# The last layer of a three-block kernel on 256 instead of 272 tokens

## The reference

```
h = jnp.concatenate([meta, x], axis=1)
for layer in range(DEPTH):                       # DEPTH = 2
    g = norm_gains[layer]
    h = h + 0.5 * rmsnorm_3(swiglu(rmsnorm_3(h, g[0]), w_ffn_in[layer, 0], w_ffn_out[layer, 0]), g[1])
    hn = rmsnorm_3(h, g[2])
    if layer < N_A_LAYERS:
        mix = gla_mixer(...)
    else:
        mix = swa_mixer(hn, swa_w_q[b], swa_sinks[b], swa_w_out[b], k_sh, v_sh, cos, sin)
    h = h + rmsnorm_3(mix, g[3])
    h = h + 0.5 * rmsnorm_3(swiglu(rmsnorm_3(h, g[4]), w_ffn_in[layer, 1], w_ffn_out[layer, 1]), g[5])
    if layer == N_A_LAYERS - 1:
        k_sh, v_sh = shared_kv(h, kv_norm, w_kv, cos, sin)
return h[:, N_META:]
```

## Time and profile before

| | |
|---|---|
| time, median of 3 runs | 3398.8 us (3395.87, 3398.80, 3410.93) |
| profiled execution, span from first to last instruction | 3401.5 us |
| PE, weight loads, DVE, ACT, POOL busy | 96%, 92%, 52%, 45%, 27% of the span |
| chain that ended last | PE 85%, DVE 7%, ACT 4% |
| mean granted clock of TensorE | 0.975 of full speed |
| HBM read | 479 MB, 141 GB/s over the span |

### The profile page before, as it was taken

The page is one execution under the profiler, slowest core; times in us unless marked ns, Lnnn a source line. Parts: engine busy times, 40 slices in busy tenths (PEclk is TensorE's granted clock), DMA queues, the critical chain, the costliest instruction groups (busy, mean ns, idle before and its releaser), DMA issues.

```text
span 3401.5 us, 65089 instructions
## 1 busy us (share of the span) xinstructions
PE 3265.4 (96%) x27906; PEld 3136.6 (92%) x27906; DVE 1780.3 (52%) x3018; ACT 1514.1 (45%) x2528; POOL 910.9 (27%) x486
## 2 busy tenths in 40 slices
PE   8998999999899999998989999999999999999999
PEld 8997999997788999988978899999889999986998
DVE  5456555548664545356576444454535446445543
ACT  5444444544323544447454544444424435443442
POOL 3321232332343322322211222233113223221222
PEclk9999999999899999999999999999999999998999
DMA  6552354554202555543433445455324544530353
GB/s 224 186 171 78 137 186 168 186 174 155 69 3 87 185 174 179 186 139 114 154 106 115 134 150 176 145 177 175 110 69 142 174 162 154 175 131 26 134 175 114
DMA packets 133391, 484.61 MB, mean 142 GB/s; under 512 B 14959, under 2 KB 17151, under 8 KB 132399
## 3 DMA queue, kind: packets, MB, share of 16 engines
q1 hardware_dynamic: 131120, 470.25, 41.1%
q0 software_dynamic: 1984, 10.19, 0.9%
HBM read 479.34 MB, written 1.05 MB: 141 GB/s over the span
## 4 chain that ended last, share of the span: by engine, by line
PE 85%; DVE 7%; ACT 4%; issue 2%; POOL 1%; DMA 0%; SPq 0%; DVEq 0%; ACTq 0%; POOLq 0%
PE ps L182 84%; DVE lo L159 1%; ACT arena L179 1%; ACT hi L179 1%; PE ps L190 1%; DVE tmp L167 1%; DVE arena L159 1%; ACT L179 1%; DVE arena L167 1%; DVE yT L167 1%; POOL small L159 0%; ACT hh L179 0%; DVE xT L159 0%; DVE small L176 0%; POOL arena L159 0%
## 5 line engine op out<-in xcount | busy, mean ns | idle before, releaser
L182 PE MATMUL ps<-hh,lo 128*128 128x256 f32 (+1 forms) x4624 | 1313.2, 286 | 0.0
L182 PE MATMUL ps<-hh,hi 128*128 128x256 f32 (+1 forms) x4336 | 1240.9, 289 | 31.3 <-DVE hl L167 8.8
L182 PE MATMUL ps<-hl,hi 128*128 128x256 f32 (+1 forms) x4336 | 1197.2, 286 | 1.2 <-DVE hl L159 1.2
L159 POOL TENSOR_TENSOR lo<-raw,hi 128x1024 fp32r<-128x1024 f32 x271 | 689.4, 2544 | 1800.3 <-ACT hi L179 1800.1
L179 ACT ACTIVATE hi<-raw 128x1024 fp32r<-128x1024 f32 x814 | 852.2, 1051 | 440.6 <-PE ps L182 326.4
L159 DVE TENSOR_TENSOR lo<-raw,hi 128x1024 fp32r<-128x1024 f32 x543 | 700.1, 1293 | 551.8 <-ACT hi L179 531.4
L182 PEld LDWEIGHTS ps<-hh,lo 128*128 128x128 f32 x4624 | 884.8, 191 | 0.0
L182 PEld LDWEIGHTS ps<-hh,hi 128*128 128x128 f32 x4336 | 830.6, 192 | 43.6 <-ACT arena L179 12.4
L182 PEld LDWEIGHTS ps<-hl,hi 128*128 128x128 f32 x4336 | 809.1, 191 | 1.6 <-DVE hl L159 1.4
L182 PE MATMUL ps<-hfh,lo 128*128 128x256 f32 (+1 forms) x1760 | 499.0, 284 | 0.0
L182 PE MATMUL ps<-hfh,hi 128*128 128x256 f32 (+1 forms) x1520 | 430.8, 283 | 0.0
(11 more groups left out here) (366 smaller groups left out, 3939.6 us busy)
## 6 DMA issues: line engine op xcount, KB each, us to landing
raw<-in_l_ffn_w_gate SPq DMA_DIRECT2D x88, 512.0 KB, 3.5
raw<-in_l_ffn_w_up SPq DMA_DIRECT2D x88, 512.0 KB, 3.6
raw<-in_l_ffn_w_down SPq DMA_DIRECT2D x88, 512.0 KB, 3.5
raw<-in_g SPq DMA_DIRECT2D x88, 512.0 KB, 3.5
raw<-in_u SPq DMA_DIRECT2D x88, 512.0 KB, 3.5
raw<-in_d SPq DMA_DIRECT2D x88, 512.0 KB, 3.5
raw<-in_ffn_w_gate SPq DMA_DIRECT2D x44, 512.0 KB, 3.4
raw<-in_ffn_w_up SPq DMA_DIRECT2D x44, 512.0 KB, 3.5
```

The lines of the kernel that those rows point to most:

```text
L159: return self.e.tensor_tensor(o, a, b, op)
L182: return self.e.matmul(o, a, b, start=first, stop=final, skip_group_check=loose)
```

## The change

The three last stages run with T = 256. `K.T`, which the exit norms read when they are made, is set to 256 for them. The sixteen-row attention of `Swa`, with its buffers, semaphores and waits, is gone. `Rope` gets its width as an argument: `Shared` keeps 272, and the keys and values of the learned rows are still computed. The norm that `ffn3(1, 0)` takes over from `Shared` keeps 272 columns, too.

```diff
     def scale(self, act):
         act.wait_ge(*self.norm.spr(0))
-        act.act(self.K.rstd[:, 2, 0:self.T], self.norm.out, ACT.Copy).then_inc(self.rs.h, 1)
+        act.act(self.K.rstd[:, 2, 0:self.norm.T], self.norm.out, ACT.Copy).then_inc(self.rs.h, 1)
...
-        pe.mm(bank[:, 0:T3], self.K.c("turn"), src).then_inc(self.rm.h, 1)
+        pe.mm(bank[:, 0:self.T], self.K.c("turn"), src).then_inc(self.rm.h, 1)
...
-        self.rope = Rope(K, 2, "sh", K.sig)
+        self.rope = Rope(K, 2, "sh", K.sig, T)
...
-        sg, T = K.own, T3
+        sg, T = K.own, T1
...
-        K, ps, T = self.K, self.K.ps, T3
+        K, ps, T = self.K, self.K.ps, T1
...
-            if i == 14:
-                self.meta_scores(pe)
-            if i == 17:
-                self.meta_turn(pe)
-            if i == 19:
-                self.meta_values(pe)
         pe.wait_ge(*self.ol(15))
-        pe.wait_ge(*self.m8(0))
...
-            if i == 15:
-                act.wait_ge(*self.m2(0))
-                act.act(self.st2[2], self.st2[2], ACT.Exp)
-                act.act(self.S2[0:16], self.S2[0:16], ACT.Exp).then_inc(self.m3.h, 1)
...
-        act.act(self.qs[:, j % 4, :], bank[:, 0:T3], ACT.Copy, scale=0.125).then_inc(self.rope.qs.h, 1)
+        act.act(self.qs[:, j % 4, :], bank[:, 0:T1], ACT.Copy, scale=0.125).then_inc(self.rope.qs.h, 1)
...
-            if i == 16:
-                self.meta_probs(dve)
...
-            if i == 14:
-                self.meta_max(dve)
-        dve.wait_ge(*self.mh(0))
-        dve.tt(self.mix[1][:, :, T1:T3], ps[7][:, 256:384].rearrange("p (u t) -> p u t", u=8),
-               self.mix[0][:, :, T1:T3].bitcast(F32), ALU.subtract).then_inc(self.m8.h, 1)
...
-        return Ffn(K, T3, f"g3_{a}{b}", f"u3_{a}{b}", f"d3_{a}{b}", entry(K, T3, prev, "norm_gains_3", a * 6 + 4 * b),
+        T = K.T = T1 if a else T3
+        return Ffn(K, T, f"g3_{a}{b}", f"u3_{a}{b}", f"d3_{a}{b}", entry(K, T, prev, "norm_gains_3", a * 6 + 4 * b),
                    rms("norm_gains_3", a * 6 + 4 * b + 1, True, True))
...
-        lambda p: Swa(K, Lazy(K, T3, p, "norm_gains_3", 8, False), rms("norm_gains_3", 9, False, False, K.Hf)),
+        lambda p: Swa(K, Lazy(K, T1, p, "norm_gains_3", 8, False), rms("norm_gains_3", 9, False, False, K.Hf)),
```

More of the change, by code:

```diff
@@ L3704, with __init__ @@
 class Rope:
-    def __init__(self, K, n, name, sig):
-        self.K = K
+    def __init__(self, K, n, name, sig, T):
+        self.K, self.T = K, T
         self.qs, self.rm, self.t1, self.t2 = [sig(name + "_" + s, n) for s in ("in", "rot", "cos", "sin")]
@@ L3720, in dve @@
         dve.wait_ge(*self.rm(j))
-        dve.tt(t2, bank[:, 0:T3], sin, ALU.mult).then_inc(self.t2.h, 1)
+        dve.tt(t2, bank[:, 0:self.T], sin, ALU.mult).then_inc(self.t2.h, 1)
         dve.wait_ge(*self.t2(j))
@@ L3885, in __init__ @@
         self.t1, self.t2 = buf(4 * T, 4, T), buf(2 * T, 2, T)
-        self.S2, self.P2 = buf(256, 16, 16), buf(256, 16, 16)
         self.mix = (K.sqR, K.over("swal", K.pos[0], 8, T))
@@ L3889, in __init__ @@
         self.kD, self.V = K.kD3, K.V3
-        self.rope = Rope(K, 8, "sw", sg)
+        self.rope = Rope(K, 8, "sw", sg, T)
         self.rq, self.tb = sg("sw_q", 8), sg("sw_tab", 1)
@@ L3895, in __init__ @@
             K.sig(x, 16) for x in ("scores", "rowmax", "exps", "probs", "turned", "pta", "pv", "oh", "ol")]
-        (self.m0, self.m1, self.m2, self.m3, self.m4, self.m5, self.m6, self.m7, self.m8, self.mh) = [
-            sg("sw_m" + str(i), 1) for i in range(10)]
         self.st = [(K.small[:, 64 + 4 * w:66 + 4 * w], K.small[:, 66 + 4 * w:68 + 4 * w]) for w in range(16)]
-        self.st2 = [K.small[0:16, 320 + 16 * x:336 + 16 * x] for x in range(3)]
         self.down = Down(K, T, "swa_out", self.mix, 8, lambda k: self.ol(2 * k + 1), spare=spare)
@@ L3951, in product @@
         return self.K.ps[6 + j % 2 if j < 4 else 7]
[L3953 to L3981, removed]
     def scores(self, pe, w):
@@ L4038, in act @@
     def act(self, act):
-        K, W, ps, T = self.K, self.K.W, self.K.ps, T3
+        K, W, ps, T = self.K, self.K.W, self.K.ps, T1
         self.entry.act(act)
@@ L4096, in dve @@
         dve.wait_ge(*self.entry.norm.spr(0))
-        dve.mark(dve.tt(self.cos, K.c("cos"), self.entry.norm.out, ALU.mult))
-        dve.tt(self.sin, K.c("sin"), self.entry.norm.out, ALU.mult).then_inc(self.tb.h, 1)
+        dve.mark(dve.tt(self.cos, K.c("cos")[:, 0:T], self.entry.norm.out, ALU.mult))
+        dve.tt(self.sin, K.c("sin")[:, 0:T], self.entry.norm.out, ALU.mult).then_inc(self.tb.h, 1)
         dve.wait_ge(*self.tb(0))
@@ L4168, in probs @@
         dve.tt(s, s, bc(den, 144), ALU.mult).then_inc(self.pr.h, 1)
[L4170 to L4194, removed]
     def pool(self, pool):
```

## The result

The changed kernel takes 3362.77 us (median of 4 runs, 3358.51 to 3369.05), the kernel before 3400.36 us (4 runs). The ratio is 0.9896, with a 95% interval of 0.9877 to 0.9916: 1.0% faster, 35 us by the ratio. A second measurement on another occasion gave 0.9898 (0.9878 to 0.9918). The profiled span is 3361.2 us, 40.3 us less than before.

A forecast was written before the change was run, and what follows sets the result against it. PE was taken as the bound, by the distance between matmul starts; 13.8 + 16.7 + 8.9 + 0.3 = 39.7 us off the 3398.8 us median gives 3359.1, with one microsecond less gain 3360 us; range 3349 to 3371.

The forecast's parts named there:

- Width of the wide matmuls: Three late stages: a matmul of 272 columns costs 7.5 ns more than one of 256; 26.6 us over 3552 matmuls.
- The estimate of 2.1 ns: Gain per wide matmul for sixteen columns, from the skill's 81 ns at 128 and 131 at 512 columns; time 3379 us.
- Width hardly pays: Rival: the pair of weight load and matmul sets the distance, not the columns; 3387 us, chance 0.02.
- Stage (1,0): Feed-forward stage behind the shared keys and values: 11.9 us width, 0.4 sums, 1.5 exit; 13.8 us shorter.
- Stage (1,1): Last feed-forward stage: 16.7 us shorter, from its 256-token twin in the first block, 193.85 against 210.52 us.
- the last 1.8 us: Stage (1,1): rest of 16.7 us beyond parts summing to 14.9, mostly a clock dip behind the 24 small entry sums.
- Attention stage: Sliding-window attention: 3.3 width, 0.8 entry sums, 0.9 chain, 1.9 exit, 2.0 sixteen-row part; 8.9 us shorter.
- the 3.90 us: Attention entry: DVE's first addition shows no progress while POOL works; said to stay, up to 3.9 us more if gone.
- The sixteen-row part: Separate attention of the sixteen rows: scores 0.6, transposes nothing, value products 1.2, last DVE operation 0.2; 2.0 us.
- Exit and projection: End of the attention stage: exit 1.9 us shorter, 192 output-projection matmuls each 7.5 ns cheaper.
- Clock: Attention stage: removed scores may add time at 1.2 GHz, at most 2.5 us; rival of more frequent falls 3364 us, chance 0.09.
- Supply: Late feed-forward stages: weight supply keeps up at 118 ns; rival that it takes over 3384 us, chance 0.02.

The follow-up runs named there:

- experiment 1: Against the kernel before: only the last feed-forward stage at 256 tokens, stage (1,0) and attention at 272; 3378.75 us, ratio 0.9948.
- experiment 2: Against the kernel before: both late feed-forward stages at 256 tokens, attention kept at 272 with its sixteen-row part; 3370.02 us, ratio 0.9926.
- experiment 4: Changed kernel with wide matmuls of 240 columns in stage (1,0) and 192 in (1,1), one execution; 112.2 ns per matmul at both, attention stage 128.4 us.
- experiment 5: Changed kernel with wide matmuls of 128 columns in stage (1,0) and 64 in (1,1), one execution; 3502.5 us.
- experiment 3: Against the kernel before: the sixteen-row attention left out, all widths kept at 272; ratio 1.0014.
- experiment 7: Changed kernel with holding matmuls on PE before the transposes in the last steps of the attention loop; 3353.88 us, ratio 0.9874.

## Why the prediction was right, step by step

The forecast was 3360 us with 3349 to 3371; measured 3362.8. The sum of 39.7 us stands against 40.3 in the span, but its parts did not all come out, and the closeness of the total is in part luck.

*Width of the wide matmuls: right.* 7.5 ns each, in both stages and in experiments 1 and 2. The estimate of 2.1 ns that the prediction worked out from the Trainium skill, "TensorE: Matmul & The Clock Gate", section "Back-to-back issue gap", is refuted between 256 and 272 columns only; experiments 4 and 5 show a floor of PE's own just below, at 112 ns (and at 128 columns 111.7 ns, where the prediction cites 81). "Width hardly pays" would have been right for a cut from 240 columns on.

*Stage (1,0): right,* 13.8 us forecast and 13.8 measured.

*Stage (1,1): right in size, its smallest part misread.* 16.63 us against 16.7. I had put the last 1.8 us down mostly to a dip of the clock behind the 24 small sums. Experiment 3 has these 24 sums with no dip, and its stage takes 209.84 us to the first update in place of 210.52. The dip is worth 0.7 us. Another part belongs to POOL's two powers. The chain of waits of the kernel of experiment 3, at the entry of its last stage:

```profile
3197.09 3.42 POOL small L159 x2
...
3200.55 3.50 PE ps L182 x24
```

They last 3.42 us while DVE forms weight corrections, and PE, not slowed by the dip, waits for them by 0.57 us. With 256 tokens there is one power and PE's rows show no wait behind it. The dip had only hidden this wait. That is 0.7 and 0.6 of the 1.8 us; the last 0.5 us no row here places.

*Attention stage: too small,* 8.9 us forecast and 12.6 measured. That lies just outside the 5 to 12 us that the prediction had set as the sign of being right here. One term was mis-sized: the 3.90 us in which DVE's first addition shows no progress were to stay. In the changed kernel they are gone at that place, and 2.00 us of such a stretch stand three additions later. DVE's rows of the changed kernel in order of time:

```profile
3038.68 0.86 DVE L159 TENSOR_TENSOR arena<-arena 128x256 f32<-128x256 f32 x1 [1.11 <-POOL arena L159]
...
3041.64 2.11 DVE L159 TENSOR_TENSOR arena<-arena 128x256 f32<-128x256 f32 x1
```

So the fourth rotation came 5.9 us earlier within the stage (18.6 in place of 24.5 us) against 2.5 expected; at the first turned tile 5.1 us are left. I had named up to 3.9 us for this and excluded it, with the reason that POOL issues the same work; experiment 2 shows that the same work can end the other way. At the level of the stage it gave 2.5 us there. The sixteen-row part had 2.0 us; experiment 3 measures 2.6, with the transposes at nothing and the value products at 1.2 as forecast, and the scores at 1.1 in place of 0.6. Exit and projection gave 3.1 us against 3.4. Some of the 12.6 us is no gain of the change at all: the stage has 41.0 us at 1.2 GHz in this trace and had 47.8 before. By the price of such stretches in experiments 1 and 4 (6.7 us for 17.1, 8.5 us for 23.9) that is an estimated 2.5 us.

*Clock: right as a doubt, its size missed and its cause left open.* The fall comes at the steps behind the last scores, where PE waits 0.88 us per step for ACT, and lasts anything from nothing to 27 us. With the same instructions in this stage it was 27.3 and 10.2 us (before, experiment 1), and 23.9, 23.9 and nothing (changed kernel twice, experiment 4). It costs 8.5 us: 137.0 against 128.4 us. The prediction priced only what the change might add, at most 2.5 us, and not this spread between executions. Experiment 7 shows, by the clock of all its runs, that filling the waits keeps the clock up more; experiment 4 shows that the waits alone do not always bring the fall. What else decides is not shown. Whether the removed scores matter is open too: no in the trace of experiment 3, perhaps by the clock of its ten runs.

*Unchanged part:* nothing was forecast, and it took 3.1 us more. This and the 3.7 us by which the attention stage gained more than forecast nearly cancel in the total, which is closer to the forecast than the steps deserve.

*Supply:* right. No wait for weights appears between the matmuls at 118 ns, nor at 112.

## What to carry to other kernels

Before cutting columns from a dense stream of matmuls, read the distance of starts at the old and at the new width, best in a stage of the same trace that already has the new one, and find the floor under it: here the cut from 272 to 256 paid 7.5 ns, the next sixteen 6.0, and those behind them nothing. A whole twin stage, first matmul to first update, gives the term better than a sum of parts. Where an engine that sets the pace waits a little in every step, price the clock of that stretch before its instructions, and from more than one trace: the late fall alone makes 8.5 us of the attention stage, with the same instructions, where the whole change had taken 12.6. With the waits filled the stage took 127.7 us, and the whole kernel was about 8 us faster than the changed one by the ratios (0.9874 against 0.9898).

## What was not expected of the hardware

- The distance of fp32r matmuls with their own 128 x 128 weights: 125.7 ns at 272 columns, 118.2 at 256, 112.2 at 240 and 192, 111.7 at 128, all at 2.4 GHz. At 64 columns it was 112 ns too, until the clock fell 2.5 us into the stage; it then stayed at 1.2 GHz for 356 us, with 213.7 ns from start to start and PE shown as busy for all of the time in the window from 3300 to 3400 us.
- Two instructions on DVE and POOL that both read two operands from SBUF shut each other out for whole instructions: one DVE addition of 0.44 us lasted 4.64 us behind three products and a weight correction of POOL in three traces, or 0.91 us with the same neighbours in a fourth. This agrees with the Trainium skill, "SBUF — State Buffer", section "SBUF: two separate sides", which calls the pair of ports that the two engines share an exclusive lock, held for the whole instruction; the 4.64 us add that the waiting engine may lose at several boundaries in a row. What decides whether it loses is not shown.
